# Gates, branch splits and modulation moved around the merges of a two-layer hybrid transformer on one Trainium2 core

## What is computed

```python
for l in range(2):
    mod = silu(c) @ w_mod[l] + b_mod[l]           # the same for c_ctx: shifts, scales, gates
    h = modulate(rms_norm(x, g_norm1[l]), sh1, sc1)
    # w_in[l]: 8 GQA heads, 4 differential heads, GLU input u of the convolution
    y_a = gqa(h) @ w_a
    y_b = rms_norm(diff_attention(h), g_subln) * (1 - lam) @ w_b
    u = depthwise_conv31(a * sigmoid(g)) + b_dw    # 512 channels, 31 taps
    y_c = silu(layer_norm(u)) @ w_c
    g_a, g_b, g_c = split(sigmoid(h @ w_gate + b_gate))
    x = x + gt1 * ((g_a * y_a + g_b * y_b + g_c * y_c) @ w_out)
    x = x + gt2 * swiglu(modulate(rms_norm(x, g_norm2[l]), sh2, sc2))
```

## Time and profile before

| | |
|---|---|
| median of three executions | 2765.39 us (2762.3 to 2768.44) |
| the profiled execution | 2768.71 us, its span 2766.8 us |
| PE, weight loads | busy 2485.3 us (90%), 2211.2 us (80%) |
| DVE, ACT, POOL | busy 1214.9 us (44%), 1150.5 us (42%), 1019.4 us (37%) |
| mean granted PE clock | 0.955 of full speed |
| HBM traffic | 75 GB/s over the span |

### The profile page before, as it was taken

How to read it: one execution, slowest core, us unless ns; L and a number is a source line. 1 busy time by engine, 2 the same in 40 slices (tenths; PEclk the granted TensorE clock), 3 DMA queues, 4 the chain that set the end, 5 groups by cost and what they waited for, 6 DMA issues and landing times.

```text
span 2766.8 us, 34285 instructions
## 1 busy us (share of the span) xinstructions
PE 2485.3 (90%) x13556; PEld 2211.2 (80%) x13556; DVE 1214.9 (44%) x1810; ACT 1150.5 (42%) x2256; POOL 1019.4 (37%) x771
## 2 busy tenths in 40 slices
PE   5999888789988998999999998888877869899998
PEld 2888777679987997999999996777666657688887
DVE  3566555578994233111111125764457982311111
ACT  4555566643334335322331226655653233432222
POOL 1201111058883533544552232111113535444443
PEclk9999999889998998999999998999988989999999
DMA  5100111023332422332332121111101214233332
GB/s 203 51 24 24 31 31 39 12 72 120 119 116 80 163 77 69 107 99 77 115 101 68 58 73 61 31 31 38 39 16 54 84 50 133 78 98 99 99 92 91
DMA packets 62077, 209.02 MB, mean 76 GB/s; under 512 B 7392, under 2 KB 7648, under 8 KB 61664
## 3 DMA queue, kind: packets, MB, share of 16 engines
q1 hardware_dynamic: 61920, 206.84, 23.8%
HBM read 202.62 MB, written 4.19 MB: 75 GB/s over the span
## 4 chain that ended last, share of the span: by engine, by line
PE 45%; DVE 10%; ACT 5%; issue 1%; POOL 0%; ACTq 0%; DVEq 0%
PE acc L477 14%; PE acc L478 14%; PE acc L479 14%; DVE X L1491 5%; ACT M L792 2%; DVE M L1181 2%; DVE RB L1181 1%; PE sco L536 1%; PE aux L599 1%; ACT H L792 1%; DVE NM L1224 1%; ACT WHI L788 1%; PE sco L586 1%; ACT RB L792 1%; ACT R L792 0%
## 5 line engine op out<-in xcount | busy, mean ns | idle before, releaser
L401 POOL TENSOR_TENSOR WLO<-STG,WHI 128x512 fp32r<-128x512 f32 (+1 forms) x760 | 1015.4, 1362 | 1724.2 <-ACT WHI L788 1724.1
L477 PE MATMUL acc<-H,WHI 128*128 128x384 f32 (+2 forms) x2528 | 926.3, 366 | 94.8 <-ACT M L792 44.2
L478 PE MATMUL acc<-H,WHI 128*128 128x384 f32 (+2 forms) x2528 | 904.2, 358 | 0.0
L479 PE MATMUL acc<-H,WLO 128*128 128x384 f32 (+2 forms) x2528 | 903.3, 357 | 0.0
L788 ACT ACTIVATE WHI<-STG 128x512 fp32r<-128x512 f32 (+1 forms) x760 | 410.3, 591 | 628.3 <-PE acc L479 405.7
L477 PEld LDWEIGHTS acc<-H,WHI 128*128 128x128 f32 x2528 | 488.8, 193 | 155.7 <-issue 66.6
L479 PEld LDWEIGHTS acc<-H,WLO 128*128 128x128 f32 x2528 | 489.5, 194 | 33.6
L478 PEld LDWEIGHTS acc<-H,WHI 128*128 128x128 f32 x2528 | 490.5, 194 | 30.2
L1491 DVE SCALAR_TENSOR_TENSOR X<-U,WDW,X 128x783 f32<-128x783 f32 (+1 forms) x256 | 336.7, 1315 | 14.8 <-ACT X L792 6.9
L477 PE MATMUL acc<-RB,WHI 128*128 128x384 f32 (+1 forms) x816 | 291.8, 358 | 24.0 <-DVE T L1181 11.2
L1181 DVE TENSOR_TENSOR T<-G,acc 128x384 f32<-128x384 f32 (+1 forms) x114 | 68.2, 599 | 528.2 <-PE acc L479 524.6
(11 more groups left out here) (112 smaller groups left out, 2352.4 us busy)
## 6 DMA issues: line engine op xcount, KB each, us to landing
STG<-in_w_fi SPq DMA_DIRECT2D x88, 512.0 KB, 3.5
STG<-in_w_mod SPq DMA_DIRECT2D x80, 512.0 KB, 3.5
STG<-in_w_in SPq DMA_DIRECT2D x52, 512.0 KB, 3.5
STG<-in_w_gate SPq DMA_DIRECT2D x48, 512.0 KB, 3.5
STG<-in_w_fo SPq DMA_DIRECT2D x32, 512.0 KB, 3.5
STG<-in_w_br SPq DMA_DIRECT2D x48, 256.0 KB, 2.6
FIRST<-in_w_mod SPq DMA_DIRECT2D x8, 1024.0 KB, 18.6
STG<-in_w_out SPq DMA_DIRECT2D x16, 512.0 KB, 3.6
```

Of the source, the lines that this page charges most:

```text
L401: nc.gpsimd.tensor_tensor(WLO[:, s, a:a + w], STG[:, g, a:a + w], WHI[:, s, a:a + w].bitcast(F32), ALU.subtract).then_inc(S("w_split"), 1)
L477: nc.tensor.matmul(dst, lh, rh, start=first, stop=False)
L478: nc.tensor.matmul(dst, lh, rl, start=False, stop=False)
L479: return nc.tensor.matmul(dst, ll, rh, start=False, stop=last)
```

## The change

It does five things, in both layers unless one is named:

1. **Gates ahead, in the last head.** The last head now has a fill of its own (`(0, "gate")`, `(1, "gate")`): the gate tiles of branch 0, columns 0 to 3. ACT evacuates them with the bias alone (Identity) into the free half of M, and applies one sigmoid per column later (`presig`). The remaining gates go to the two banks `aux` and no longer share `acc` with the branches.
2. **Splits as memory comes free.** The chunks of the attention output are split one by one during the last head (0 to 4) and in the first columns of branch 0 (5 to 7), into places of RB in the order in which the attention leaves them (PAIR and HOME). The copies that start the convolution's sums move too, two of them into the last head.
3. **Taps spread unevenly.** 31 instead of 32 taps a channel chunk: 124 in all, of them 10 (layer 0) and 4 (layer 1) in the last head, then 3 or 4 in each of the four columns without a gate tile, 8 or 9 in the others.
4. **Gates ahead, in the convolution's norm.** In layer 0 the gate tiles (2, 1) and (2, 0) and two modulation groups, in layer 1 (2, 1), (2, 2) and (2, 0) stand between branch 1 and branch tile (2, 0), with the two sums of the norm inside them. Branch 2 has the other gates alone.
5. **Modulation moved.** Branches 0 and 1 of layer 0 have no groups any more (before: 16). Two are in the norm, two in each column of branch 2 (16), and all 22 parts of the FFN have one (before: 16 of them). After branch 2 the mark `mdone` is gone: M is split chunk by chunk, the first four before the last merge.

```diff
+EARLY = 4
+AHEAD = [(1,), (1, 2)]
+HEAD_TAPS = [[0, 0, 0, 0, 5, 5], [0, 0, 0, 4]]
+MERGE_TAPS = [[3] * 4 + [8] * 6 + [9] * 6, [4] * 4 + [8] * 4 + [9] * 8]
+MERGE_MODS = 2
...
+def merge_order(l):
+    mods = lambda k: [("mod", q, None) for _ in range(k) for q in range(2)] if l == 0 else []
+    order = [("gate", 0, j) for j in range(EARLY)]
+    for b in range(2):
+        for j in range(KC):
+            order += [("gate", b, j)] if b or j >= EARLY else []
+            order += [("branch", b, j)]
+    order += mods(2) + [("gate", 2, j) for j in AHEAD[l]] + [("gate", 2, 0)]
+    for j in range(KC):
+        order += mods(MERGE_MODS // 2)
+        order += [("gate", 2, j)] if j and j not in AHEAD[l] else []
+        order += mods(MERGE_MODS // 2) + [("branch", 2, j)]
+    return order
...
@@ tensor: between branch 1 and branch 2, and branch 2
+                if l == 0:
+                    mod_groups(l, 1)
+                    conv_sums(l, 0)
+                    mod_groups(l, 1)
+                    gate_tile(l, 2, 1, between=lambda: conv_sums(l, 1), where=(1, 0))
+                else:
+                    gate_tile(l, 2, 1, between=lambda: conv_sums(l, 0), where=(0, 4))
+                    gate_tile(l, 2, 2, between=lambda: conv_sums(l, 1), where=(0, 6))
+                gate_tile(l, 2, 0, between=turn_pending)
+                for j in range(KC):
+                    before = c.at("turn")
+                    mod_groups(l, MERGE_MODS // 2)
+                    if j and j not in AHEAD[l]:
+                        gate_tile(l, 2, j, between=turn_pending)
+                    else:
+                        turn_pending()
+                    mod_groups(l, MERGE_MODS // 2)
+                    branch_tile(l, 2, j)
@@ scalar: the same stretch in layer 0
+                if l == 0:
+                    mod_group(l)                  # hi(), hi(), mod_row()
+                    exp_set()
+                    for ch in range(CC):
+                        conv_square(l, ch)
+                    mod_group(l)
+                    hi()
+                    gate_ahead(l, 1, 0)
+                    conv_root(l)
+                    gate_ahead(l, 1, 1)
...
+                for ch in range(CC):
+                    conv_out(l, ch)
+                    if ch == 0:
+                        hi()
+                gate(l, 2, 0)
...
@@ vector: branches 0 and 1, end of branch 2
                 for b in range(2):
-                    for c2 in range(2):
-                        for q in range(4):
-                            for t in range(TAPS4):
...
-                            if mod_here(l, b=b) and (b or c2 or q):
-                                mod_group(c2 * 4 + q + (MOD_FIRST + b * KC) - 1)
-                            merge(b, c2 * 4 + q)
+                    for j in range(KC):
+                        conv_taps(l, MERGE_TAPS[l][KC * b + j])
+                        merge(b, j)
+                        if b == 0 and j < 3:
+                            branch_lo(l, 5 + j)
...
                 for j in range(KC):
-                    if mod_here(l, b=2):
-                        mod_group(j + (MOD_FIRST + 2 * KC) - 1)
+                    mod_groups(at["turned", l, j])
+                    if j == KC - 1:
+                        for k in range(4):
+                            merged_lo(k)
                     merge(2, j)
```

More of the change, by code:

```diff
@@ L483, in wait_half, with tile @@
                 pe.wait_ge(S("w_split"), 2 * c.at("tile") + (h + 1))
-            def tile(kn, moving, rngs, ready=None, between=None, name=None):
+            def tile(kn, moving, rngs, ready=None, between=None, name=None, where=None, gate=False):
                 s = c.at("tile") % SLOTS
+                where = where or (len(rngs) - 1, kn // 2)
                 for n, (a, w) in enumerate(rngs):
-                    dst = open_acc()
+                    dst = open_aux() if gate else open_acc()
                     for k in range(kn):
@@ L917, in slot @@
                                 exp_set()
-                        if done and (j, t) != (HEADS - 1, "g"):
+                        if done:
                             hi()
@@ L1119, in _ @@
-                c.step("mdone", 1)
-                act.wait_ge(S("mdone"), c.at("mdone"))
-                for k in range(KC):
-                    fn(H[:, 0, k, 0:n], MM[:, k, 0:n], ACT.Copy, sem="mhi")
+                for b in range(2):
+                    for j in range(KC):
+                        if b or j >= EARLY:
+                            hi()
+                            gate(l, b, j)
+                        hi()
+                        if b == 0 and j < EARLY:
+                            for i in ([0, 1] if j == 0 else [j + 1] if j + 1 < EARLY else []):
+                                bank, before = banks["acc"][at[(l, HEADS, f"m{i}"), nr(l) - 1]]
+                                act.wait_ge(S(f"acc_free{bank}"), before + 2)
+                                fn(MM[:, 4 + i, 0:n], MM[:, 4 + i, 0:n], ACT.Sigmoid, sem="presig")
+                            if j < 3:
+                                branch_hi(l, 5 + j)
+                            if j < 2:
+                                conv_bias(l, 2 + j)
@@ new lines, in _ @@
+                for ch in range(CC):
+                    conv_out(l, ch)
+                    if ch == 0:
+                        hi()
+                gate(l, 2, 0)
+                ahead = slice(CC * XW, CC * XW + len(AHEAD[l]) * n)
+                bank, before = banks["aux"][at[(l, 2, AHEAD[l][-1], "gate"), nr(l) - 1]]
+                act.wait_ge(S(f"aux_free{bank}"), before + 2)
+                fn(X1[:, ahead], X1[:, ahead], ACT.Sigmoid, sem="presig2")
+                for j in range(KC):
+                    for _ in range(MERGE_MODS // 2):
+                        mod_group(l)
+                    if j and j not in AHEAD[l]:
+                        hi()
+                        gate(l, 2, j)
+                    for _ in range(MERGE_MODS // 2):
+                        mod_group(l)
+                    hi()
```

394 lines of the change are left out of this document (238 added, 156 removed).

## The result

Before 2763.1 us (20 runs, 2759.2 to 2769.8), after 2771.3 (20 runs, 2764.1 to 2777.3): ratio **1.0027**, 95% interval 1.0019 to 1.0035. Measured once more with the experiments it was 1.0034 (1.0021 to 1.0046). So the change costs 8 us; forecast was a gain of 16.

The account below looks back on a forecast made before the run. PE, busy for 90% of the span, was taken as the bound, with DVE the busy one in branches 0 and 1. Terms: +13.2 - 1.7 - 27.5 = -16, so 2750 us; own range 2738 to 2763, with rivals 2712 to 2777.

Parts of the forecast that it names:

- Branches 0 and 1 of layer 0: Merges of layer 0: DVE bounds them with 152 us of taps and ends at 771 instead of 825; 56 us won.
- The norm: Convolution's norm of layer 0: second sum 5.4 us later; gate tile (2, 0) ends 46.9 us after the last branch tile.
- the columns of branch 2 in layer 0 and what follows them: Weight loop sets a 20 us pitch; w_out runs effectively from 977.4, before 979.1; 1.7 us won.
- rival B: Weight loop takes 8.0 us, not 6.7, because ACT's `hi()` stands behind other work: 2776 us, chance 0.14.
- Layer 1: Last head to branch 2 of layer 1: merges start at 2095, 17 us won by DVE's end, 27.5 us in all.
- Rival D: Layer 1's last head grows by 10 us of its 21.8, ACT's evacuations lengthening the softmax chain: 2760 us, chance 0.13.
- FFN: Third part of layer 0's FFN gets 6 more modulation groups at 2.2 us on a PE without gaps: +13.2 us.
- PE fills its idle time in a head: Layer 0's last head: idle PE hides four gate tiles, which would cost 33.4 us without that cover.

Follow-up runs that it names:

- experiment 1: Changed kernel with only the modulation move undone (groups back in branches 0 and 1, none in the FFN's third part): 2764.6 us, 0.9996 of before.
- experiment 3: Changed kernel with two steps of layer 0's convolution norm reordered (ACT's splits ahead of the squares, DVE's group sum earlier): 2762.7 us, 0.9990 of before.
- experiment 2: Changed kernel with each weight tile loaded by two DMAs of half a tile: 2759.8 us, 0.9980 of before.
- kernel 7: The kernel before the change, with each weight tile loaded by two DMAs of half a tile: 2765.3 us, 1.0006 of before.
- experiment 6: Changed kernel with ACT's bias copy of the first convolution channel one item earlier in layer 1's last head: 2771.8 us, 1.0025 of before.
- 5: Changed kernel with no gate tiles made ahead in layer 1's last head, its merge taps spread 7 or 8 per column: 2774.5 us, 1.0034 of before.
- 9: Changed kernel with no gate tiles made ahead in layer 0's last head, its merge taps spread 7 or 8 per column: 2775.6 us, 1.0035 of before.
- 10: Changed kernel with gate tile (2, 1) of layer 0 made in its branch 2 column, not ahead in the norm: 2770.8 us, 1.0020 of before.

## Why the prediction was wrong

The direction was wrong. Forecast was -16: +11.5 in layer 0, -27.5 in layer 1. The landmarks give +26 and -22, in sum +4 (+5 against before alone), the medians +8. Point by point:

- **Branches 0 and 1 of layer 0: right.** "DVE ends at 771"; it ended at 775.5, 2.9 of the 4.5 us being a later start (585.9 for 583). PE ran further ahead than forecast: its last branch tile ended at 760.9, not 769. The mean tap of the group was forecast at 1.33 (152 us over 114 taps, gaps in it), measured 1.31. The rule of the Trainium skill ("SBUF — State Buffer", section "SBUF: two separate sides") on DVE and GpSimd excluding each other agrees with this trace: by start times and durations, the 57 taps of layer 0 that no split of POOL overlaps take 1.02 to 1.04 us each, the 67 that one overlaps 1.51 in the mean. Half of the taps take no more than 1.036 us in the row below, where before the median was 1.397, and a mean of 1.6 came back with the modulation in experiment 1.

```profile
L1447 DVE SCALAR_TENSOR_TENSOR X<-U,WDW,X x115: 1022/1036/2058, 582.2 to 772.1; 128x783 f32<-128x783 f32 x115
```

- **The norm: right.** "The norm gets 5.4 us later": 6.1, and for the reason given (experiment 3). "The tile ends at t = 46.9", at 815.9 with the branch's end at 769; it ended at 820.6, the 4.5 us being those of the step before.
- **The step that failed most: the columns of branch 2 in layer 0 and what follows them.** The prediction took "3 x 6.7 = 20 us" and a w_out "effectively at 977.4". Measured: 21.1 a column, and w_out effectively at 990.7 (988.73 and 2.0 us that its first matmuls lose at a granted clock of 0.50; the prediction's "2.3 of stalls" before are the same, at 0.61 from 976.8 to 981.0). Of these 13.3 us, 4.7 come with the norm, 0.5 in the gateless columns, 5.9 in the five columns (PE starts its gate tiles at 856.5 and, last, at 962.4) and 2.2 in the last column and the tail. The mechanism was right, by experiments 1, 2 and 7: the weight loop sets the pitch, and did not before. The term was mis-sized, a loop of 7.04 us in the mean for 6.7, taken from one pair of rows of a loop with nothing in its way. The excess is what rival B named, ACT taking up tiles late, but B put the loop at 8.0; the truth lies between the two, and so does the time. Of the 20 us between the forecast (-16) and the landmarks (+4), 13.3 are here, 5.5 in layer 1 and 1.1 in the FFN.
- **Layer 1: half a step failed.** "DVE starts the merges at 2095", 49 us after the head's start; it was 55. The four taps and the low halves of chunks 3 and 4 wait for ACT in turn (experiment 6). So E won 8, not 17. The norm and branch 2 did as well as forecast: F won 10.5, against 10.5 (15 against kernel 7). The taps themselves came as sized: 1.05 us where 126 / 120 was forecast. In sum 20 to 22 won, not 27.5. Rival D had the late start (10 us of it) and a time of 2760.
- **FFN: right.** +13.2 forecast, +14.3 measured.

The medians lie 4 us further up than the landmarks of two profiles each add up to. No experiment says where; C, which alone varies by 5 us from profile to profile, is the likeliest place, but that was only argued.

Behind the terms stands a choice. The prediction priced the removal of 16 groups from the branches at a gain, the return of ten in branch 2 at the loop's time and six in the FFN at 13.2. The experiments price each: moving the groups loses 9 us (1), gates ahead in the heads are worth nothing that the runs can tell (5, 9), the one in the norm of layer 0 brings nothing (10). What wins in layer 1 (20 to 22 us) was not taken apart by a run, but the two profiles say where it stands. DVE begins the taps of the merges there as late as before (55.2 us behind the head's start, 53.8 in the second profile, against 55.3) with eight fewer to do, four made in the head and four zero taps dropped: at 1.05 us each that is the 8 of E. In F the third merge of branch 2 begins 32.1 us behind the last tap (ended at 2267.3) instead of 41.9 (ended at 2256.1), since columns 1 and 2 have their gates already. The changed kernel and before, DVE in order of time:

```profile
2299.47 1.10 DVE L1340 TENSOR_TENSOR M<-M,T 128x512 f32<-128x512 f32 x1
...
2298.03 0.69 DVE L1181 TENSOR_TENSOR M<-M,T 128x512 f32<-128x512 f32 x1
```

Read so, the gates made ahead in the norm of layer 1 win, where the columns behind have PE's pitch of 8.16 us, and the one in layer 0, ahead of columns at the weight loop's pitch, does not. One more edit is in the diff and not in the list of the change: DVE centres the convolution's channels one by one and ACT squares each at once, so that the first square stands 3.6 us behind the first sum instead of 5.8 in layer 0, 2.5 instead of 4.2 in layer 1. No run has it alone.

That PE fills its idle time in a head was true and worth little, because DVE with its taps was due at the same time behind it.

## What to carry to other kernels

Price a piece of work in each place where it could stand, by what ends last there, before moving it: here the same modulation group costs 2.4 us where only PE is busy, 3.9 beside the taps and 5.4 where the weight supply is at its limit. A supply loop gives tiles per time, whatever an engine makes of a tile, so many tiles with little work in them are the wrong thing to gather in one stretch; and a loop time is to be taken as the mean of many, since with no slack each late one counts. Filling an engine's idle time wins only if no second engine is due at the same point. And a time that comes out unchanged can be a gain and a loss of the same size: here experiment 1 hid 20 us won in one layer and 18 lost in the other.

## What the runs showed of the hardware

POOL pays for the taps as well as DVE for the splits. POOL's group of the 128x512 split (busy us, mean ns, idle before), in branches 0 and 1 of experiment 1:

```profile
L442 POOL TENSOR_TENSOR WLO<-STG,WHI 128x512 fp32r<-128x512 f32 x92 | 156.0, 1716 | 43.1 <-ACT WHI L872 43.0
```

And of the changed kernel, in branches 0 and 1 of layer 0, then in its branch 2, without taps:

```profile
L440 POOL TENSOR_TENSOR WLO<-STG,WHI 128x512 fp32r<-128x512 f32 x32 | 58.6, 1851 | 34.0 <-ACT WHI L865 34.0
...
L440 POOL TENSOR_TENSOR WLO<-STG,WHI 128x512 fp32r<-128x512 f32 x51 | 65.8, 1315 | 17.4 <-ACT WHI L865 17.1
```

1.72 and 1.85 us beside taps, 1.32 without. The prediction charged the taps alone. A column with 3 full tiles and one branch tile beside eight taps holds POOL for 3 x 3.4 + 2.7 = 13 of its 16.0 us in experiment 1, so moving modulation back loads POOL as well as DVE. And a load of half the size doesn't land in half the time. The profile page's row of the modulation tiles, KB and median us from issue to landing, in the changed kernel:

```profile
STG<-in_w_mod SPq DMA_DIRECT2D x80, 512.0 KB, 3.5
```

And in experiment 2:

```profile
STG<-in_w_mod SPq DMA_DIRECT2D x160, 256.0 KB, 2.9
```
